# A transformer kernel's opening: x in two transfers, a shorter warm-up, and more products ahead of the next rows of w_ada

## The reference

```python
c_act = jax.nn.silu(c)
ada = c_act @ w_ada[l] + b_ada[l]                       # 1024 x 6144
sh_m, sc_m, g_m, sh_f, sc_f, g_f = jnp.split(ada, N_ADA, axis=-1)
h = modulate(rmsnorm(x, norm_mix_g[l]), sh_m, sc_m)     # rmsnorm(x, g) * (1 + scale) + shift
proj = h @ w_in
```

## Time and profile before

| | |
|---|---|
| time, median of 3 runs | 1005.09 us (1004.12 to 1005.45) |
| the profiled execution: span, first to last instruction | 1002.7 us |
| PE busy | 994.2 us, 99% of the span |
| DVE busy | 719.3 us, 72% |
| ACT busy | 597.5 us, 60% |
| granted clock of TensorE | 1.00 |
| moved by DMA | 196.7 MB, mean 196 GB/s |
| DMA share from 16 to 44 us | about 1.0, 411 to 420 GB/s |

### The profile page before, as it was taken

One profiled execution on the slowest core, in us unless ns is written; L12 is line 12 of the kernel. 1 busy time (PEld: TensorE's weight loads), 2 busy tenths in 40 slices (PEclk: granted clock), 3 DMA queues, 4 the chain that ended last, 5 costly groups with the idle time before them and its releaser, 6 DMA issues.

```text
span 1002.7 us, 16654 instructions
## 1 busy us (share of the span) xinstructions
PE 994.2 (99%) x6652; PEld 893.8 (89%) x6652; DVE 719.3 (72%) x1225; ACT 597.5 (60%) x1010; POOL 0.4 (0%) x5
## 2 busy tenths in 40 slices
PE   9999999999999999999999999999999999999997
PEld 8899999998888888999999888888999899888886
DVE  5898888878888988887658555655766558565652
ACT  4778665557566666767647545554666546555452
POOL 0000000000000000000000000000000000000000
PEclk9999999999999999999999999999999999999999
DMA  9975767535656664553326555455553337655621
GB/s 368 397 252 181 265 230 286 202 136 210 209 204 226 226 232 167 213 205 126 127 89 228 197 205 204 169 183 201 215 192 135 127 105 253 203 174 178 205 81 42
DMA packets 28443, 196.72 MB, mean 196 GB/s; under 512 B 3152, under 2 KB 3664, under 8 KB 5584
## 3 DMA queue, kind: packets, MB, share of 16 engines
q1 hardware_dynamic: 28224, 195.41, 54.7%
q10 hardware_dynamic: 144, 0.26, 0.1%
HBM read 194.61 MB, written 1.05 MB: 195 GB/s over the span
## 4 chain that ended last, share of the span: by engine, by line
PE 86%; DVE 8%; ACT 4%; issue 1%; POOLq 0%; DVEq 0%; ACTq 0%
PE PS L1246 13%; PE PS L1063 8%; PE PS L1064 7%; PE PS L1065 7%; PE PS L1249 7%; PE PS L1337 6%; PE PS L1338 6%; PE PS L1339 6%; DVE wlo L1904 4%; PE PS L1216 3%; PE PS L1219 3%; PE PS L1217 3%; PE PS L1279 2%; PE PS L1280 2%; PE PS L1281 2%; PE PS L1436 2%
## 5 line engine op out<-in xcount | busy, mean ns | idle before, releaser
L1904 DVE TENSOR_TENSOR wlo<-raw,whi 128x1024 fp32r<-128x1024 f32 x306 | 358.3, 1216 | 61.6 <-ACT whi L1500 58.9
L1500 ACT ACTIVATE whi<-raw 128x1024 fp32r<-128x1024 f32 x300 | 297.9, 1047 | 59.0 <-PE PS L1339 53.5
L1246 PE MATMUL PS<-HX,whi 128*128 128x512 f32 x736 | 261.3, 398 | 0.0
L1249 PE MATMUL PS<-HX,wlo 128*128 128x256 f32 x736 | 206.6, 281 | 0.0
L1246 PEld LDWEIGHTS PS<-HX,whi 128*128 128x128 f32 x736 | 138.3, 188 | 33.9
L1063 PE MATMUL PS<-HX,whi 128*128 128x256 f32 x496 | 145.1, 293 | 1.1 <-DVE HX L1878 0.6
L1064 PE MATMUL PS<-HX,whi 128*128 128x256 f32 x496 | 140.2, 283 | 0.0
L1249 PEld LDWEIGHTS PS<-HX,wlo 128*128 128x128 f32 x736 | 139.0, 189 | 1.2
L1065 PE MATMUL PS<-HX,wlo 128*128 128x256 f32 x496 | 140.1, 282 | 0.0
L1337 PE MATMUL PS<-whi,Oh 128*128 128x512 f32 x344 | 134.8, 392 | 0.0
L1338 PE MATMUL PS<-wlo,Oh 128*128 128x512 f32 x344 | 134.2, 390 | 0.0
(11 more groups left out here) (270 smaller groups left out, 1649.6 us busy)
## 6 DMA issues: line engine op xcount, KB each, us to landing
raw<-wall SPq DMA_DIRECT2D x151, 1024.0 KB, 5.0
raw<-wada SPq DMA_DIRECT2D x18, 1024.0 KB, 5.1
raw<-wall SPq DMA_DIRECT2D x8, 512.0 KB, 16.3
GA<-wada SPq DMA_DIRECT2D x2, 1024.0 KB, 20.7
GA<-alibi SPq DMA_DIRECT2D x1, 2048.0 KB, 9.5
raw<-wall SPq DMA_DIRECT2D x2, 768.0 KB, 5.7
X<-xt SPq DMA_DIRECT2D x1, 1024.0 KB, 4.9
KM<-wada SPq DMA_DIRECT2D x1, 1024.0 KB, 14.2
```

The costliest lines, as they stand in the source:

```text
L1246: e.matmul(PS[:, b, :], whi[place(n)][:, at:at + 128], HX[:, k, :, :].rearrange("p h t -> p (h t)"), start=k == 0, stop=k == 7, skip_group ...
L1249: m = e.matmul(PS[:, b, 0:T], wlo[place(n)][:, at:at + 128], Hh[:, k, :], start=False, stop=k == 7, skip_group_check=True)
L1500: e.activation(whi[place(n)][:, c], raw[i % RAW][:, c], ACT.Copy).then_inc(*up("a_whi", (n, half)))
L1904: e.tensor_tensor(wlo[place(n)][:, c], raw[i % RAW][:, c], f32(whi[place(n)][:, c]), ALU.subtract).then_inc(*up("v_wlo", (n, half)))
```

## The change

The first transfer of x becomes two, of tiles 0 to 3 and of tiles 4 to 7, each with a semaphore of its own. The squares go by halves: of the first half ACT squares tiles 0 and 1 and DVE tiles 2 and 3, and DVE adds them; then the same for the second half. The warm-up has 14 products in place of 28, and a later one 6 in place of 4. `next_tile` for tile i + 1 gets p parts of tile i in front of `ada_rows`, with p = 2, 3, 3, 1, 0, 0 for i = 0 to 5; the two parts between `ada_rows` and `ada_columns` stay, and the rest follows. The total of all work is the same.

```diff
-    emit("warm", 28, 0)
+    emit("warm", 14, 0)
...
-    emit("warm", 4, 0)
+    emit("warm", 6, 0)
...
-        next_tile(i + 1, lambda: None, lambda: emit("slice", s, parts[0:2]))
+        p = (2, 3, 3, 1, 0, 0)[i]
+        next_tile(i + 1, lambda: emit("slice", s, parts[0:p]), lambda: emit("slice", s, parts[p:p + 2]))
...
-            emit("slice", s, parts[2:])
+            emit("slice", s, parts[p + 2:])
...
-        e.dma_start(X[:, :, :], xt).then_inc(*up("d_x", 0, 16))
+        for half in range(2):
+            e.dma_start(X[:, 4 * half:4 * half + 4, :], xt[:, 4 * half:4 * half + 4, :]).then_inc(*up(f"d_x{half}", 0, 16))
...
             elif step == "x_squares":
-                on.wait_ge("d_x", 0)
                 for g in range(2):
-                    e.activation(pair(SQ, 2 * g), pair(X, 2 * g), ACT.Square).then_inc(*up("a_sq", ("x", g)))
+                    on.wait_ge(f"d_x{g}", 0)
+                    e.activation(pair(SQ, 2 * g), pair(X, 4 * g), ACT.Square).then_inc(*up("a_sq", ("x", g)))
...
             elif step == "x_squares":
-                on.wait_ge("d_x", 0)
                 for g in range(2):
-                    e.tensor_tensor(pair(QM, 2 * g), pair(X, 4 + 2 * g), pair(X, 4 + 2 * g), ALU.mult).then_inc(
+                    on.wait_ge(f"d_x{g}", 0)
+                    e.tensor_tensor(pair(QM, 2 * g), pair(X, 4 * g + 2), pair(X, 4 * g + 2), ALU.mult).then_inc(
                         *up("v_sq", ("x", "own", g)))
-                for g in range(2):
                     on.wait_ge("a_sq", ("x", g))
                     on.wait_ge("v_sq", ("x", "own", g))
                     e.tensor_tensor(pair(SQ, 2 * g), pair(SQ, 2 * g), pair(QM, 2 * g), ALU.add).then_inc(
```

More of the change, by code:

```diff
@@ L1481, in scalar @@
         on = On(e, marks)
-        x_at = {k: ("d_x", 0) for k in range(8)}
+        x_at = {k: (f"d_x{k // 4}", 0) for k in range(8)}
         sq_free, rb_free, pt_free = {}, {}, {}
@@ L2052, in vector @@
                 on.wait_ge("a_rb", "x")
-                on.wait_ge("d_x", 0)
+                on.wait_ge(f"d_x{i // 4}", 0)
                 e.tensor_tensor(QM[:, i, :], X[:, i, :], RB[:, 0, :], ALU.mult).then_inc(*up("v_nrm", ("mix", i)))
```

## The result

| | before | after |
|---|---|---|
| time, median | 1005.09 us (1004.12 to 1005.45) | 1010.55 us (1008.98 to 1011.28) |
| span of the profiled execution | 1002.7 us | 1008.7 us |
| granted clock, mean of the span | 1.000 | 0.995 |

The ratio is 1.0054, 95% interval 1.0043 to 1.0065: 5.5 us slower, where 1.8 us had been forecast with a range up to 1008.2. The time lies outside the range. In four of the five executions the mean granted clock was 0.995 or 0.996; in the fifth it was 0.998 and the time 1008.98.

A forecast was written before the change was run, and what follows sets the result against it. PE, busy for 979.7 of 984 us from 16 us on, was taken as the bound. 2.76 us won in the opening against 4.52 lost from S to row step 5 gave 1005.09 + 1.8 = 1006.9 us, range 1004.9 to 1008.2.

The forecast's parts named there:

- The length of the chain: From a tile's row step through ACT's copy, PE's turn and DVE's work to that tile's start on PE: at least 4.27 us.
- The sum: The forecast's addition up to row step 5: 2.76 us won in the opening against 4.52 lost after it, 1.8 later.
- S: The time PE starts tile 0: 15.94 us before, forecast at 13.18 after.
- row step 5: PE's 16 recorded products of c with the rows of w_ada for tile 5: 32.02 us before, forecast at 33.78.
- Nothing gives it back behind row step 5: In the rest of the kernel the code is unchanged and PE idles only 4.3 us, so the 1.8 us loss stays.
- Row step 0 at 8.70: In the opening, PE's products of c with the w_ada rows for tile 0 start at 8.70 us, not 11.46.
- the 2.76: The us won in the opening by the earlier row step for tile 0, from x in halves and the shorter warm-up.
- rival 2: PE's clock falls in its stands before tile 0 and in the next 16 us: 2.6 us on top, 1009.5; chance 7%.
- Rival 1: The products in front of the row steps cover a wait, PE bound by its own work: 1004.0 us, 0.1% faster; 12%.
- rival 4: The 1.8 us loss is given back behind row step 5, in waits that don't move with PE: 1005.1 us; 8%.
- Rival 3: Both halves of x land together at about 6.07 us, or the first is slowed: 2.7 us later, 1007.8; chance 13%.

The follow-up runs named there:

- the filled kernel: The changed kernel with 18 first warm-up products in place of 14, and 5 more between the two pairs of sums of squares: 1008.77 us, ratio 1.0039.

## Why the prediction was wrong

- **The length of the chain and the parts in front: right.** The sum had 4.52 for S to row step 5 and its stalls; the parts alone cost 4.5, S to row step 5 is 20.57 against 20.60 forecast, and the stands of 0.64, 0.99 and 1.00 are a little under the 0.7, 1.1 and 1.1.
- **Nothing gives it back behind row step 5: right.** 5.97 at the chunk behind the slices, 6.0 in the span.
- **Row step 0 at 8.70: wrong, and this is the step that failed.** It rested on two halves landing at 4.7 and 6.1, "since SP's queue serves in order". They were used at 5.87 and 8.12. The bounds that I set for the first half, 3.6 to 6.07, held it, but the second half was allowed only 0.45 beyond the whole's landing, the price of one more issue; it took 2.0. The sum also took the landing of the block for tile 0, 8.64, from before; it landed at 10.6, so 8.70 was out of reach by the block alone. With the clock held, row step 0 comes at 11.1 (the filled kernel), so of the 2.76 only 0.3 is left, or 0.8 with the halves as early as in the changed kernel's own trace.
- **The clock: rival 2 in kind, at another place.** I had priced it at the stand ahead of tile 0, 1.2, and given it 7%. It fell with the stands of 0.87 and 1.13 ahead of the sums, which the shorter warm-up laid bare and the late second half made longer. Behind it lies an omission: the sum itself had PE idle for 0.3 between the two pairs of sums, and I looked for stands only from the end of the second warm-up on. It costs 1.8 to 2.3, against the 2.6 of the rival. In the kernel with the shorter warm-up alone a stand of 1.66 lets the clock fall in 7 executions of 10, so 7% was far too little for a stand of a kind that the trace of before doesn't have.
- **The sum, with the terms as measured:** 4.5 for the parts and row step 1, less 0.3 won at row step 0, plus 1.8 for the clock, is 6.0; the span grew by 6.0, the median by 5.5. The last two terms are read off the same pair of traces, so their adding up proves neither of them alone (0.8 and 2.3 add up as well).
- **Rival 1 (the parts cover a wait) and rival 4 (given back) have nothing for them. Rival 3 (the halves land together)** was nearest for the transfers, but not right: the halves landed apart, the first a little earlier than it assumed and the second 2 us later. Its 1007.8 is the time of the changed kernel with x whole and the clock held (1007.85 and 1008.05).

## What to carry to other kernels

Before work is moved in front of a request whose answer comes back through other engines, measure that round trip and add up what is left behind the request to cover it, the next request included; work moved ahead is work taken from the cover. A warm-up is worth its length up to the point where the engine would otherwise stand: here 22 products, which end just behind the first sum of squares, kept the clock up in all executions, and 14 didn't. And a transfer cut in two doesn't bring its first half at half the time: look at the landing of both, and of the transfers behind them, before work is ordered by halves.

## What the runs showed of the hardware

- Two transfers of 512 KB at the head of the queue bring 1 MB 1.1 us later than one (used at 7.22 against 6.12 with nothing behind them, one execution each), and 1.9 to 2.7 later with transfers behind; halves by partitions 2.8, quarters 2.6. The rate from 4 to 5 us was 283 in place of 418 GB/s, and 152 to 254 with transfers behind. The transfers behind them land late as well: the block for tile 0 at 10.6 in place of 8.64.
- TensorE's clock fell from 2.4 to 1.2 GHz around or soon after stands of 0.87 and 1.13 us, of 0.27 and 1.38, of 1.54 and 0.29, of 1.66, and of 1.44, all within the first 12 us, and after one of 3.16 that ended at 18.36. PE was busy for most of what followed, and the lower level lasted 6.8 us all the same (3.4 in the last case). Stands of 1.44 that ended at 10.70 (x in quarters) and of 1.57 that ended at 16.34 (parts in front alone) left it at 1.00. The same program can go either way from one execution to the next. What tells these cases apart the runs don't show.
- The column of the granted clock misses the slow start: in the kernel before it stands at 1.00 from the first us, while PE does 6 or 7 recorded warm-up products a us from 2 to 6 us and 11 to 12 from then on. Six or seven a us is the pace of the stretches at 0.50 later, so at the start the level has to be read from the spacing.
